# Down projection of a two-block transformer: where the sums of weight quadrants are formed

## The reference, cut to what matters

```python
D_FF = 2816
def swiglu(h, w_gu, w_down):
    gu = jnp.einsum('bsd,df->bsf', h, w_gu)
    g, up = gu[..., :D_FF], gu[..., D_FF:]
    return jnp.einsum('bsf,fd->bsd', jax.nn.silu(g) * up, w_down)

for l in range(2):
    ...
    h = layer_norm(ALPHA * h + mix, ln1_g[l], ln1_b[l])
    h = layer_norm(ALPHA * h + swiglu(h, w_gu[l], w_down[l]), ln2_g[l], ln2_b[l])
```

## Time and profile before

| what | value |
|---|---|
| time, median of 3 (lowest, highest) | 1986.66 us (1982.17, 1986.81) |
| time of the profiled execution | 1983.29 us |
| its span, first to last instruction | 1981.9 us |
| TensorE busy | 1804.9 us (91%) |
| VectorE / ScalarE / GpSimd busy | 1048.4 / 812.8 / 556.9 us |
| mean granted TensorE clock | 0.963 of full |
| gate and up part, layer 1 | 11 iterations of 21.76 us |

### The profile page before, as it was taken

The page is one execution under the profiler, slowest core; times in us unless marked ns, Lnnn a source line. Parts: engine busy times, 40 slices in busy tenths (PEclk is TensorE's granted clock), DMA queues, the critical chain, the costliest instruction groups (busy, mean ns, idle before and its releaser), DMA issues.

```text
span 1981.9 us, 26809 instructions
## 1 busy us (share of the span) xinstructions
PE 1804.9 (91%) x10264; PEld 1425.2 (72%) x10264; DVE 1048.4 (53%) x2009; ACT 812.8 (41%) x1462; POOL 556.9 (28%) x616
## 2 busy tenths in 40 slices
PE   7999999996998764998999999988998999999985
PEld 6888777785554434776888888877776788888874
DVE  4558776663311016968454333666868454333666
ACT  3344476321433234666242222445566242222443
POOL 1029155102222211233010044740233010034642
PEclk9999999996999996998999999999998999999998
DMA  4334200576999983211323232993211223323891
GB/s 163 87 109 128 96 2 2 170 290 238 387 385 398 397 328 127 75 55 44 106 76 96 96 96 96 221 221 89 63 65 43 93 78 96 100 92 105 211 221 59
DMA packets 155813, 287.50 MB, mean 145 GB/s; under 512 B 13088, under 2 KB 109984, under 8 KB 143392
## 3 DMA queue, kind: packets, MB, share of 16 engines
q1 hardware_dynamic: 119024, 229.92, 33.2%
q0 software_dynamic: 23776, 31.47, 8.3%
q10 hardware_dynamic: 12880, 24.33, 3.5%
HBM read 277.29 MB, written 16.78 MB: 148 GB/s over the span
## 4 chain that ended last, share of the span: by engine, by line
PE 49%; DMA 12%; DVE 9%; issue 3%; ACT 2%; POOL 1%; PEld 1%; PEldq 0%; POOLq 0%; ACTq 0%; DVEq 0%; SPq 0%
PE b L595 14%; PE b L596 14%; PE b L597 14%; DMA m<-in_w_gate_up 7%; DMA m<-in_w_down 4%; PE b L2144 3%; PE b L2697 2%; DVE m L2872 1%; PE b L2169 1%; PE b L2679 1%; DVE m L581 1%; PE b L2665 1%; DMA m<-in_w_in 1%; DVE m L805 1%; DVE m L747 1%
## 5 line engine op out<-in xcount | busy, mean ns | idle before, releaser
L595 PE MATMUL b<-m,m 128*128 128x512 f32 (+3 forms) x2016 | 765.4, 380 | 37.5 <-DVE m L581 28.6
L596 PE MATMUL b<-m,m 128*128 128x512 f32 (+3 forms) x2016 | 755.9, 375 | 0.0
L597 PE MATMUL b<-m,m 128*128 128x512 f32 (+3 forms) x2016 | 755.5, 375 | 0.0
L581 DVE TENSOR_TENSOR m<-m,m 128x1024 fp32r<-128x1024 f32 (+1 forms) x252 | 309.3, 1233 | 419.3 <-ACT m L571 418.0
L595 PEld LDWEIGHTS b<-m,m 128*128 128x128 f32 x2016 | 385.2, 191 | 113.2 <-issue 36.2
L571 ACT ACTIVATE m<-m 128x1024 fp32r<-128x1024 f32 (+2 forms) x276 | 282.0, 1027 | 419.4 <-PE b L597 343.0
L597 PEld LDWEIGHTS b<-m,m 128*128 128x128 f32 x2016 | 384.7, 191 | 65.2
L596 PEld LDWEIGHTS b<-m,m 128*128 128x128 f32 x2016 | 385.4, 191 | 62.4
L2144 PE MATMUL b<-m,m 128*64 128x256 f32 x1024 | 125.2, 387 | 27.1 <-DMA m<-in_w_gate_up 25.7
L2144 PEld LDWEIGHTS b<-m,m 128*64 128x64 f32 x1024 | 72.9, 138 | 77.8 <-issue 37.2
L3297 POOL TENSOR_TENSOR m<-m,m 128x256 fp32r<-128x256 f32 x44 | 60.6, 1388 | 241.1 <-ACT m L3118 241.1
(11 more groups left out here) (353 smaller groups left out, 2079.6 us busy)
## 6 DMA issues: line engine op xcount, KB each, us to landing
m<-in_w_gate_up SPq DMA_DIRECT2D x64, 1024.0 KB, 30.2
m<-in_w_gu SPq DMA_DIRECT2D x88, 512.0 KB, 3.5
m<-in_w_down SPq DMA_DIRECT2D x32, 1024.0 KB, 30.7
m<-in_w_in SPq DMA_DIRECT2D x48, 512.0 KB, 3.7
m<-in_w_down POOLq DMA_DIRECT2D x68, 256.0 KB, 9.4
m<-in_w_down SPq DMA_DIRECT2D x30, 512.0 KB, 6.8
m<-in_w_in SPq DMA_DIRECT2D x20, 448.0 KB, 3.6
m<-in_w_o SPq DMA_DIRECT2D x16, 512.0 KB, 3.7
```

The source lines that it names most:

```text
L581: e.tensor_tensor(split(wlo[HX[i]], i), source(i), fr(split(whi[HX[i]], i)), ALU.subtract).then_inc(sem("w_lo"), 1)
L595: e.matmul(out, xh, yh, start=start, stop=False, skip_group_check=True)
L596: e.matmul(out, xh, yl, start=False, stop=False, skip_group_check=True)
L597: return e.matmul(out, xl, yh, start=False, stop=stop, skip_group_check=True)
```

## The change

The accumulating transfers, the held places and the special cases for them go. `gpsimd_down` issues no transfer any more, and all 42 chunks of the down part pass through the four raw places. Three products out of seven load quadrants of `w_down` (q = 0, 1, 4); the other four load sums from four new DRAM tensors per layer.

These sums are formed in the gate and up part, in six groups g of rows (groups 0 to 4 are two rows of 128, group 5 is one). SyncE loads the four quadrants of a group to free SBUF, VectorE adds them in four turns, each of which waits for the one before, and SyncE stores the four results. Group g is added in iteration g: two turns between the two products silu x up, two after `settle`; group 5 follows group 4 in iteration 4. A group's loads wait for all stores of the group before (group 5 has places of its own, those of the gain and bias that `settle` used). The wait of groups 4 and 5 is for both groups' loads. ScalarE's copy k = 11 now waits for the 24 stores instead of for `settle`, and so does the load of product 2's weights.

```diff
-DN_FIRST = ((1, 0), (0, 0), (0, 1), (1, 1), (1, 1), (0, 1), (1, 0))
-DN_KIND = ("raw", "held", "sum", "sum", "raw", "pair", "sum")
-DN_SECOND = {2: (0, 1), 3: (1, 1), 5: (1, 1), 6: (1, 0)}
+DN_FROM = ((1, 0), (0, 0), 0, 1, (1, 1), 2, 3)
+DN_QUADS = ((0, 0), (0, 1), (1, 1), (1, 0))
...
+        WS = [[nc.dram_tensor(f"s_ws{l}{n}", [P, 11, 512], F32).ap() for n in range(4)] for l in range(2)]
...
+        def load_quads(e, l, g):
+            wd = io["w_down_2"][l].rearrange("(k p) n -> p k n", p=P)
+            n = min(2, 11 - 2 * g)
+            if g == 0:
+                e.wait_ge(*at("w_used", CH[f"gu{l}"] + 1))
+                e.wait_ge(*at("ff_s", 22 * l + 1))
+            elif g == 5:
+                e.wait_ge(*at("ln_ov", 8 * l + 8))
+            else:
+                e.wait_ge(*at("ws_out", 16 * sums_before(l, g)))
+            for x, (kq, fq) in enumerate(DN_QUADS):
+                k, f = 11 * kq + 2 * g, 512 * fq
+                e.dma_start(sum_rows(g)[x], wd[:, k:k + n, f:f + 512]).then_inc(sem(f"ws_in{x}"), 16)
+
+        def store_sums(e, l, g):
+            n = min(2, 11 - 2 * g)
+            for turn, x in enumerate((0, 1, 2, 3)):
+                e.wait_ge(*at("ws_add", sums_before(l, g, turn + 1)))
+                e.dma_start(WS[l][(0, 2, 1, 3)[x]][:, 2 * g:2 * g + n, :], sum_rows(g)[x]).then_inc(sem("ws_out"), 16)
+
+        def add_quads(e, l, g, turns):
+            for turn in turns:
+                out, other = ((0, 1), (1, 2), (2, 0), (3, 2))[turn]
+                for x in (out, other):
+                    e.wait_ge(*at(f"ws_in{x}", 16 * (6 * l + (6 if g >= 4 else g + 1))))
+                if turn:
+                    e.wait_ge(*at("ws_add", sums_before(l, g, turn)))
+                a, b = sum_rows(g)[out], sum_rows(g)[other]
+                e.tensor_tensor(a, a, b, ALU.add).then_inc(sem("ws_add"), 1)
+
+        def load_layer(e, l, first):
+            gu, dn = CH[f"gu{l}"], CH[f"dn{l}"]
+            for g in range(5):
+                i = gu + 4 * g + 8
+                load_chunks(e, first, i)
+                load_quads(e, l, g)
+                if g == 4:
+                    load_quads(e, l, 5)
+                load_chunks(e, i, i + 2)
+                store_sums(e, l, g)
+                if g == 4:
+                    store_sums(e, l, 5)
+                first = i + 2
+            load_chunks(e, first, dn + 12)
+            e.wait_ge(*at("ws_out", 16 * 24 * (l + 1)))
+            load_chunks(e, dn + 12, dn + 42)
...
                     if k == 11:
-                        e.wait_ge(*at("ln_ov", 8 * l + 8))
+                        e.wait_ge(*at("ws_out", 16 * 24 * (l + 1)))
...
                     e.tensor_tensor(FR[:, 2 * i + f, :], bank[o + 2 + f][:, :], SL[f], ALU.mult).then_inc(sem("ff_u"), 1)
+                    if f == 0 and i < 5:
+                        add_quads(e, l, i, (0, 1))
                 if i < 4:
...
                     settle(e, 1 + 2 * l, i, gO, bO)
+                if i < 5:
+                    add_quads(e, l, i, (2, 3))
+                if i == 4:
+                    add_quads(e, l, 5, (0, 1, 2, 3))
...
         def gpsimd_down(e, l):
-            c0, u = CH[f"dn{l}"], 2 + 2 * l
-            for q, before in ((2, 1), (3, 2), (6, 3)):
-                for c in range(6):
-                    e.wait_ge(*at("w_lo", halved_by(c0 + 6 * before + c)))
-                    for kk in range(chunks[c0 + 6 * q + c][1]):
-                        e.dma_start(held_rows(c, kk), halves_of(ADDED[c0 + 6 * q + c], kk), accum_op=ALU.add).then_inc(sem(f"w_sum{c}"), 16)
-            for c in range(6):
-                cell, of, n_landed = RX[c0 + 30 + c]
-                e.wait_ge(*at(f"w_raw{of}", n_landed))
-                e.dma_start(view(raw[cell], c0 + 30 + c), ADDED[c0 + 30 + c], accum_op=ALU.add).then_inc(sem(f"w_sum{c}"), 16)
+            u = 2 + 2 * l
```

More of the change, by code:

```diff
@@ L140, in weight_chunks @@
         at[f"dn{l}"] = len(chunks)
-        for q, (kq, fq) in enumerate(DN_FIRST):
+        for src in DN_FROM:
             for c in range(6):
[L143 to L149, removed]
+                n = min(2, 11 - 2 * c)
+                if isinstance(src, int):
+                    chunks.append((io["sums"][l][src][:, 2 * c:2 * c + n, :], n, 512))
+                else:
+                    k, f = 11 * src[0] + 2 * c, 512 * src[1]
+                    chunks.append((wd[:, k:k + n, f:f + 512], n, 512))
+    return chunks, at, twins
 SINGLES = [(0,), (1,), (2,), (3,)]
@@ L154, with raw_places @@
 PAIRS = [(4, 5), (6, 7), (8, 9), (30, 31), (10, 11), (12, 13), (14, 15), (0, 1), (2, 3), (16, 17), (18, 19), (20, 21), (22, 23), (24, 25), (26, 27), (28, 29)]
-def raw_places(n, first, end, kinds):
+def raw_places(n, first, end):
     loads, place, held, landed = [], [], {}, {}
-    i = passed = 0
+    i = 0
     while i < n:
[L163 to L171, removed]
+        cells = PAIRS[(i - first) // 2 % len(PAIRS)] if first <= i < end else SINGLES[i % RAW]
         loads.append((i, cells, max((held[c] for c in cells if c in held), default=None)))
@@ L247, in build_program @@
         Y2 = nc.dram_tensor("s_y2", [2 * S, D], F32).ap()
-        chunks, CH, twins, KIND, ADDED = weight_chunks(io)
+        WS = [[nc.dram_tensor(f"s_ws{l}{n}", [P, 11, 512], F32).ap() for n in range(4)] for l in range(2)]
+        chunks, CH, twins = weight_chunks({**io, "sums": WS})
         WHOLE = range(CH["up0"], CH["mix0"])
-        LOADS, RX, landed = raw_places(len(chunks), CH["up0"], CH["mix0"], KIND)
+        LOADS, RX, landed = raw_places(len(chunks), CH["up0"], CH["mix0"])
         HX, HB = halves_places(len(chunks), (CH["gu0"], CH["mix1"], CH["gu1"]), WHOLE)
@@ L255, in build_program @@
             goes_on[m] = (a, ATT[a] + 16 * landed[cell])
-        for c, cell in enumerate((4, 6, 8, 10, 12, 14)):
-            goes_on[f"w_held{c}"] = (f"w_raw{cell}", 16 * landed[cell])
+        for name, cell in (("ws_in0", 4), ("ws_in1", 6), ("ws_in2", 8), ("ws_in3", 10), ("ws_add", 12), ("ws_out", 14)):
+            goes_on[name] = (f"w_raw{cell}", 16 * landed[cell])
         def halved_by(i):
@@ L456, in build_program @@
         SL = [M.f(512) for _ in range(2)]
-        M.pos = XS
-        WT = M.f(6, 256)
+        WA4 = []
+        for pos, end in ((DA0, EE0), (EE0 + 2048, XS), (EE0 + 3072, XS), (XS + 1024, UU0)):
+            M.pos = pos
+            WA4.append(M.f(2, 512))
+            assert M.pos <= end
+        M.pos = EE0
+        WA1 = [M.f(1, 512) for _ in range(4)]
         M.pos = UU0
@@ L488, in load_chunks @@
                     continue
[L489 to L496, removed]
                 if before in WHOLE:
@@ L530, in held_in @@
[L530 to L547, removed]
@@ L2373, in sync_gains @@
         def sync_gains(e):
-            last = max(i for i, cells, _ in LOADS if cells and cells[0] in (TAIL + 4, GAINS))
+            last = max(i for i, cells, _ in LOADS if cells[0] in (TAIL + 4, GAINS))
             e.wait_ge(*at("w_used", last + 2))
@@ L3402, in sync_program @@
             sync_final(e)
-            load_chunks(e, CH["mix0"] + RAW, len(chunks))
+            load_layer(e, 0, CH["mix0"] + RAW)
+            load_layer(e, 1, CH["mix1"])
             sync_out(e)
```

34 lines of the change are left out of this document (10 added, 24 removed).

## The result

The changed kernel takes 1962.94 us (median of 4 runs, 1959.25 to 1964.31) against 1984.41 us of the kernel before beside it: 21.5 us less, a ratio of 0.9891 with a 95% interval of [0.9867, 0.9915]. The forecast was 20.7 us less and 1966.0. The profiled execution took 1964.31 us, its span is 1962.7 us, 19.2 under the span before.

What follows compares the result with a forecast made beforehand. It took the down part's DMA queue, filled by accumulating transfers (share 1.19 at 216 GB/s), to stall TensorE. 24.1 us go, 3.4 come: 20.7 less, from 1986.7 to 1966.0 us; range for 8 in 10, 1958 to 1979.

Steps and rivals of the forecast that it cites:

- The stalls of products 5 and 6: Down part, first two TensorE stops per layer plus lower-clock restarts: all go with plain loads, 11.1 and 11.5, together 22.6 us.
- The ring as the only supply: Down part: plain loads through four raw places keep up, landing in 3.5 us with 5 us of room; DMA share 0.5 to 0.6.
- rival 2: Down part keeps half of its stalls because VectorE, at 12.12 of 15 us, becomes what TensorE waits for: 1977.5; 12%.
- Additions in iterations 0 to 3: Gate and up part: VectorE's four additions just fit before the wanted low half, room 0.35; cost 0.1 each, 0.8 us.
- Iteration 4: Gate and up part: group 5's second quadrant lands 1 us late, stalling TensorE 1.3 per layer (0 to 3.5), 2.6 us.
- The third stops: Down part, ahead of the last three chunks: stops stay in kind but shrink by 1.0 and 0.5 us, partly backlog.
- The way through DRAM: Gate and up part: stores land in 2.6 us, quadrants come in time in iterations 1 to 3, room about 2 us.
- rival 3: Gate and up part: stores then loads in one queue come late and VectorE waits for quadrants; slower, 2014; 7%.

Runs made afterwards that it cites:

- experiment 2: Kernel before with GpSimd's 39 transfers per layer plain instead of accumulating, same number, order and waits (sums left out): 1965.85 us, ratio 0.9906.
- experiment 3: Changed kernel with own semaphores for group 5's four loads, so group 4's additions wait for group 4's loads alone: 1957.02 us, ratio 0.9858.
- experiment 4: Changed kernel with VectorE's block of the down part's iteration (6, 4) moved behind the last low half (6, 5): 1952.40 us, ratio 0.9848.
- experiment 5: Changed kernel with TensorE waiting for each of product 6's last three chunks where first needed, not all at once: 1956.92 us, ratio 0.9864.
- Experiment 7: Changed kernel with each sum stored twice, the second time to an unread DRAM tensor, next loads waiting for both: 1972.51 us, ratio 0.9944.
- experiments 6: Changed kernel with the last addition of each group made twice, one VectorE instruction more per group: 1976.80 us, ratio 0.9969.
- experiment 1: Changed kernel with the sums taken out: no quadrant loaded, added or stored in gate and up, single w_down quadrants loaded instead: 1955.92 us, ratio 0.9855.

## Why the prediction was right

- **The stalls of products 5 and 6** (22.6 us): right in place and size. None is left, and the two stretches show it. Their cause was named as the DMA cost of accumulated bytes; experiment 2 shows that for about two thirds of the idle time. The rest, from the way these transfers are issued, was not in the prediction's cause.
- **The ring as the only supply**: right. The share in the down part was put at 0.5 to 0.6 and is 0.60; VectorE at 11.83 of 15 us holds nobody up, so rival 2 is out. The loads landed later than the 3.5 us of the working, 4.5 (medians of the down part's 512 KB loads), which its 5 us of room could take.
- **Additions in iterations 0 to 3** (0.8 us): nothing was lost. The room was put at 0.35 and is 0.5. The pair of additions beside GpSimd's first L3300 takes 2.89 instead of 2.57, L751 beside the second 1.64 instead of 1.22: 0.7 in all, less than the 0.97 before. The rule of the Trainium skill that a VectorE instruction with two SBUF inputs and a GpSimd instruction that reads SBUF contend for an exclusive lock ("SBUF — State Buffer", "Who interferes with whom") agrees with the trace in kind: both slow each other. The 1.48 estimated by it is twice what was measured.
- **Iteration 4** (2.6 us in all): right in place and mechanism, too small. The wait was put at 1.0 and is 2.50 (2.47 in layer 0). What was mis-sized is how long the loads take: 10.5 us from the first of group 4 to group 5's second quadrant (1704 to 1714.5), where experiment 3's trace has 12.0 and the changed kernel 11.9 up to the first addition (1696.37 to 1708.31). The stops are 1.91 and 1.93 instead of 1.3, the periods 2.20 and 2.23 longer, 4.4 us. That group 5's loads are what is waited for is shown by experiment 3. The wait is not the same in each execution: in experiment 4, where this code is unchanged, it is 2.98 and 1.60.
- **The third stops** (1.5 us): the step "part of each is backlog from the stalls before" failed. They gave 0 and 0.37. They are VectorE's block ahead of the last low half (experiment 4) and the wait for three chunks at once (experiment 5). A stop of 0.41 in layer 1 (ahead of 1945.78, 0.6 us by the distance of starts), which the sum left out, went too, and the clock gave 1.07.
- **The way through DRAM**: the stores land in time, and no addition in iterations 1 to 3 waits for a load, so rival 3 is out. SyncE's timeline in layer 1, iteration 0, shows the last of the stores, then two w_gu loads, then group 1's quadrants:

```profile
1626.15 1.68 SPq L526 DMA_DIRECT2D s_ws<-m  x2
1628.65 1.52 SPq L496 DMA_DIRECT2D m<-in_w_gu  x2
1630.31 2.08 SPq L520 DMA_DIRECT2D m<-in_w_down  x4
```

The last store is issued by 1627.8, and the loads that wait for all four start at 1630.31, behind two others. The forecast gave a store the 2.6 us of the output's; the traces with landing times show more, experiment 3's for instance (median, us from issue to landing):

```profile
s_ws<-m SPq DMA_DIRECT2D x40, 512.0 KB, 3.4
```

That is far from the 9.6 at which the gain would be gone. The first addition of group 1 follows at 1640.45 without a wait. Experiment 7 shows where this ends: with twice the stores VectorE begins to wait in iterations 2 and 3.

The sum by terms is then 22.6 + 0.6 + 0.4 + 1.1 - 4.4 = 20.3 in the touched places, against 20.7 forecast. That the two agree so closely is in part luck. Iteration 4 (1.8 too little) and the third stops (1.1 too much) were made good by the clock, the small stop and the 0.8 set aside for iterations 0 to 3. The forecast of 1966.0 also starts from 1986.7, where the kernel before took 1984.41 beside the changed one.

## What to carry to other kernels

Accumulating transfers can be the thing that fills a DMA queue: compare share and GB/s of a stretch with those of plain loads of the same rows before taking the queue's length for a given. When work moves to an idle engine, look for the instruction behind it that the critical engine waits for, and measure the room there, not the busy share: here 64% busy left 0.5 us. A shared count for two groups of loads cost 4.4 us here, and a wait for three chunks where one is needed 4.9 us of TensorE's stops, where the whole change gains about 20. And once a stop is gone, look again at what sets the end: two repairs of the same stop did not add up in layer 1.

## What the runs showed of the hardware that was not expected

After a stop TensorE sometimes restarts at the lower clock level, and the length of the stop alone does not say whether. In the changed kernel the stop of 2.13 in layer 0 was followed by full speed, and so were those of 2.11 to 2.13 in the same place before the change and in experiments 6 and 7. In experiments 1, 2 and 3 the same stop, in the same place and as long, was followed by matmuls at the lower level, seven of them in experiment 1, 1.6 us more:

```profile
1349.63 0.77 PE L594 MATMUL b<-m,m 128*128 128x512 f32 x1 [2.13 <-DVE m L580]
...
1352.33 0.63 PE L594 MATMUL b<-m,m 128*128 128x512 f32 x1
1352.76 0.50 PE L595 MATMUL b<-m,m 128*128 128x512 f32 x1
```

All fourteen stops for a weight chunk of 3.64 to 7.02 us in these traces were followed by the lower level, at once or within two or three matmuls, at a cost of 1.3 to 2.7 us each against a restart at full speed. And a 256 KB transfer that accumulated landed in 9.4 us, the plain one in the same queue in 3.9, as the pages of the kernel before and of experiment 2 have it:

```profile
m<-in_w_down POOLq DMA_DIRECT2D x68, 256.0 KB, 9.4
```

```profile
m<-in_w_down POOLq DMA_DIRECT2D x68, 256.0 KB, 3.9
```
